# A state-space scan with decays from summed rows in DRAM, a channel-wise y, and z's weights in another slot

## The reference, cut to what matters

```python
y_f = ssd_scan(xs, dtl[:, :, 0], a[0], bf, cf, hf_ctx)
y_b = ssd_scan(xs[:, ::-1], dtl[:, ::-1, 1], a[1], bb[:, ::-1], cb[:, ::-1], hb_ctx)[:, ::-1]
y = y_f + y_b + d_skip[layer][:, None] * xs
y = y.reshape(bsz, n, D_INNER)
y_ssd = rmsnorm(y * jax.nn.silu(z), ssd_norm_w[layer]) @ w_ssd_out[layer]
```

## Time and profile before

| | us |
|---|---|
| median of 3 runs | 3327.76 (3324.04 to 3328.95) |
| span of the profiled execution | 3323.6 |
| scan's loop in it, first conv product to f_in's first | 71.40 to 739.23 |

### The profile page before, as it was taken

The page is one execution under the profiler, slowest core; times in us unless marked ns, Lnnn a source line. Parts: engine busy times, 40 slices in busy tenths (PEclk is TensorE's granted clock), DMA queues, the critical chain, the costliest instruction groups (busy, mean ns, idle before and its releaser), DMA issues.

```text
span 3323.6 us, 40435 instructions
## 1 busy us (share of the span) xinstructions
PE 3186.9 (96%) x13834; PEld 1884.2 (57%) x13835; DVE 1355.6 (41%) x2174; ACT 730.8 (22%) x1302; POOL 393.2 (12%) x312
## 2 busy tenths in 40 slices
PE   7999999999999999999999999999899999999999
PEld 5555555556488743333333333333587788888887
DVE  2544545464434532122221222212457477555451
ACT  3212131312021111111111111111314354311100
POOL 0212222222100100000000000000201244100000
PEclk9999999999999999999999999999899999999999
DMA  4121212134612369999999999879412121222111
GB/s 203 56 77 57 76 52 81 47 107 160 218 73 76 137 258 374 384 394 388 393 382 381 392 389 355 324 285 368 147 51 105 42 78 56 86 76 89 64 76 54
DMA packets 185079, 615.71 MB, mean 185 GB/s; under 512 B 18176, under 2 KB 55168, under 8 KB 174240
## 3 DMA queue, kind: packets, MB, share of 16 engines
q1 hardware_dynamic: 161216, 552.79, 43.6%
q0 software_dynamic: 10944, 39.85, 3.3%
q10 hardware_dynamic: 12832, 21.88, 1.8%
HBM read 578.01 MB, written 36.44 MB: 185 GB/s over the span
## 4 chain that ended last, share of the span: by engine, by line
PE 85%; DMA 6%; DVE 5%; issue 1%; ACT 1%; SPq 1%; POOL 0%; ACTq 0%; DVEq 0%; POOLq 0%
PE ps L322 24%; PE ps L2273 16%; PE ps L2247 11%; PE ps L1940 9%; PE ps L271 6%; DMA slot<-in_w_exp 5%; PE ps L2011 3%; PE ps L2502 2%; PE ps L2027 2%; PE ps L1986 2%; PE ps L2032 1%; PE ps L2474 1%; PE ps L2457 1%; PE ps L2242 1%; PE ps L2238 1%
## 5 line engine op out<-in xcount | busy, mean ns | idle before, releaser
L2273 PE MATMUL ps<-slot,xT_blk 128*64 128x512 f32 x3200 | 733.8, 599 | 28.8 <-DMA slot<-in_w_exp 26.4
L2273 PEld LDWEIGHTS ps<-slot,xT_blk 128*64 128x64 f32 x3200 | 217.9, 137 | 465.6 <-issue 376.4
L2247 PE MATMUL ps<-slot,aT 128*64 128x512 f32 x1632 | 363.8, 598 | 0.9 <-ACT aT L1638 0.9
L1940 PE MATMUL ps<-hT,slot 128*128 128x512 f32 (+1 forms) x896 | 307.6, 501 | 1.1 <-ACT small L1435 1.1
L2247 PEld LDWEIGHTS ps<-slot,aT 128*64 128x64 f32 x1632 | 117.5, 138 | 239.4 <-issue 239.4
L3007 DVE TENSOR_TENSOR gate<-ps,b_row 128x512 f32<-128x512 f32 x50 | 34.6, 692 | 513.1 <-PE ps L2273 512.6
L1940 PEld LDWEIGHTS ps<-hT,slot 128*128 128x128 f32 x896 | 168.0, 190 | 129.8 <-issue 120.9
L2628 DVE SCALAR_TENSOR_TENSOR conv<-ps,g_conv,conv 128x510 f32<-128x510 f32 (+1 forms) x224 | 133.3, 631 | 193.2 <-ACT conv L1448 189.8
L3003 DVE MEMSET b_there<- 128x1 f32 x50 | 3.0, 59 | 391.8 <-DMA b_few<-in_b_gu 383.0
L322 PE MATMUL ps<-in_t,in_s 128*128 128x264 f32 x528 | 124.7, 386 | 0.5 <-issue 0.5
L2011 PE MATMUL ps<-hT,slot 128*128 128x512 f32 x256 | 121.5, 620 | 0.0
(11 more groups left out here) (509 smaller groups left out, 4792.4 us busy)
## 6 DMA issues: line engine op xcount, KB each, us to landing
slot<-in_w_exp SPq DMA_DIRECT2D x768, 512.0 KB, 9.2
in_w<-in_w_ffn SPq DMA_DIRECT2D x22, 1024.0 KB, 4.8
expert_rows<-zero SPq DMA_DIRECT2D x4, 4608.0 KB, 22.6
slot<-in_w_xbc SPq DMA_DIRECT2D x8, 2048.0 KB, 26.4
w_modT<-in_w_modT POOLq DMA_DIRECT2D x32, 512.0 KB, 3.5
rnn_w<-in_w_rnn SPq DMA_DIRECT2D x16, 1024.0 KB, 4.8
expert_rows<-y_row ACTq DMA_DIRECT2D x102, 128.0 KB, 5.6
out_w<-in_w_ffn_out SPq DMA_DIRECT2D x8, 1408.0 KB, 8.2
```

The lines of the kernel that those rows point to most:

```text
L1940: last = pe.matmul(ps[:, 2 * (m % 2) + part, 0:n], w[:, (k * 4 + m % 4) * P:(k * 4 + m % 4 + 1) * P], hT[:, k, c0:c0 + n], start=(k == 0), ...
L2247: last = pe.matmul(ps[h * UNIT:(h + 1) * UNIT, 6, :], aT[:, t, d * UNIT:(d + 1) * UNIT], slot[4 + d][:, t * D + h * 512:t * D + (h + 1) * ...
L2273: last = pe.matmul(ps[h * UNIT:(h + 1) * UNIT, 2 * s + t, :], xT_blk[:, k, s * UNIT:(s + 1) * UNIT], slot[i // 4][:, at:at + 512], start=( ...
```

## The change

- The decays. TensorE makes, once, the running sums S as rows (8 matmuls, [64 heads x 512 tokens], step `rows`); VectorE copies them to SBUF; ScalarE's queue stores them with 8 DMAs in the DRAM tensor sum_rows. For each chunk ScalarE's queue loads one row of 1024 values to all 128 partitions (`load_sums`, 512 KB into sum_here, two buffers, two chunks ahead). GpSimd adds a mask that is 0 or -1e30 (`row`), and ScalarE takes, for each of the 8 heads, exp of 128 columns with the bias -S_s (`decay`). `segment`, da_upto and cb_masked are gone; VectorE multiplies decay by cb straight from PSUM.
- The carried term. ScalarE takes exp of sum_here in one 1024-wide instruction (`into`), VectorE multiplies it by C for all 8 heads (`scaled`).
- The output. Both terms of all 8 chunks are written by channels: for each head 64 columns of the state or of x_dt are the weights, 128 columns of c_into or decay move, and the result goes to one half of the partitions of banks 4 to 7, where the two directions and both terms are summed in PSUM. The steps on y_part and y_tok, GpSimd's skip and the 16 transposes are gone; at the end VectorE does y = x times skip + PSUM, and y times silu(z), four times each (silu of x is kept by channels in xT).
- z's weights go to the slot that conv0 to conv3 used, after conv3; z0 comes whole ahead of the states, and the rest is spread unevenly: half a tile in each of chunks 0 to 4, a quarter in 5 and 6, none in 7. The loop over groups becomes one over pairs of groups on SyncE and TensorE, as the slots alternate.
- The second direction's first two states come in chunk 3, the rest in chunk 4; scaled(j+1) and masked(j+1) follow those of j on VectorE without any y step between.

```diff
         with act.Fori(0, GROUPS) as g:
+            def load_sums(j):
+                d, _, t = CHUNKS[j]
+                act.dma_start(sum_here[j % 2][:].rearrange("p h l -> p (h l)"),
+                              sum_rows[bass.ds(g * (2 * TT) + (d * TT + t), 1), :].partition_broadcast(P)).then_inc(s_row[j % 2], 16)
+            load_sums(0)
+            load_sums(1)
...
             def decays(j):
-                ssd_pe.after(act, f"segment{j}", g)
-                ssd_act.done(act.activation(decay[j % 2][:].rearrange("p (q h) l -> p q (h l)", q=2), ps[:, 0:2, :],
-                                            ACT.Exp), f"decay{j}")
+                act.wait_ge(s_row[j % 2], g * 64 + (16 * (j // 2) + 16))
+                if j >= 2:
+                    ssd_pe.after(act, f"carried{j - 2}", g)
...
+                ssd_act.done(act.activation(c_into[j % 2][:], sum_here[j % 2][:], ACT.Exp), f"into{j}")
+                ssd_pool.after(act, f"row{j}", g)
+                for h in range(HPG):
+                    last = act.activation(decay[j % 2][:, h, :], decay[j % 2][:, h, :], ACT.Exp, bias=g_small[:, MINUS_SUM, t, d, h:h + 1])
+                ssd_act.done(last, f"decay{j}")
+                if j < 6:
+                    ssd_act.after(act, f"into{j}", g)
+                    load_sums(j + 2)
...
+            def into_y(j, left, right, first):
+                t = CHUNKS[j][2]
+                for h in range(HPG):
+                    half = slice(h % 2 * HD, (h % 2 + 1) * HD)
+                    last = pe.matmul(ps[half, Y_BANK + h // 2, t * P:(t + 1) * P], left[:, h * HD:(h + 1) * HD], right[:, h, :],
+                                     start=first, stop=True, skip_group_check=not first)
+            z_piece(0, 0, 1)
             states(0, [0, 1])
-            segment(0)
+            scores(0)
             states(0, [2, 3, 4])
             for j in range(8):
+                states(1, STATES_AT.get(j, []))
+                for piece in Z_PIECES[j]:
+                    z_piece(*piece)
+                ssd_dve.after(pe, f"scaled{j}", g)
+                ssd_dve.after(pe, f"state{d}_{i + 1}", g)
+                ssd_pe.done(into_y(j, state[:, i, :], c_into[j % 2], j == 0), f"carried{j}")
+                if j < 7:
+                    scores(j + 1)
                 ssd_dve.after(pe, f"masked{j}", g)
                 ssd_pool.after(pe, f"x_dt{d}", g)
-                for h in range(HPG):
-                    last = pe.matmul(ps[:, 6, h * HD:(h + 1) * HD], decay[j % 2][:, h, :], x_dt[:, t, h * HD:(h + 1) * HD],
...
+                ssd_pe.done(into_y(j, x_dt[:, t, :], decay[j % 2], False), f"diagonal{j}")
...
+            def weigh(j):
+                ssd_dve.done(dve.tensor_tensor(c_into[j % 2][:], c_into[j % 2][:], over_heads(cT[:, d, t * P:(t + 1) * P]), ALU.mult), f"scaled{j}")
+                ssd_pe.after(dve, f"cb{j}", g)
+                ssd_act.after(dve, f"decay{j}", g)
+                ssd_dve.done(dve.tensor_tensor(decay[j % 2][:], decay[j % 2][:], over_heads(ps[:, 2, 0:P]), ALU.mult), f"masked{j}")
+            states(0, [0, 1])
+            weigh(0)
+            states(0, [2, 3, 4])
...
+            def sums(j):
+                pool.wait_ge(s_row[j % 2], g * 64 + (16 * (j // 2) + 16))
+                if j >= 2:
+                    ssd_pe.after(pool, f"diagonal{j - 2}", g)
...
+                ssd_pool.done(pool.tensor_tensor(decay[j % 2][:], sum_here[j % 2][:],
+                                                 never[:, d, :].unsqueeze(1).broadcast_to([P, HPG, P]), ALU.add), f"row{j}")
```

More of the change, by code:

```diff
@@ L79 @@
 CHUNK = KD * 4 * P
+NEVER = -1e30
 class Steps:
@@ L629, in program @@
     zT = area("zT", [P, 4, SEQ])
+    sum_here = [area(f"sum_here{i}", [P, HPG, P]) for i in range(2)]
+    never = area("never", [P, 2, P])
     CHUNKS = [(d, i, i if d == 0 else TT - 1 - i) for d in range(2) for i in range(TT)]
@@ L1914, in _ @@
             heads = slice(d * N_HEADS, (d + 1) * N_HEADS)
-            last = pe.matmul(into_psum[:, :, heads], cst[:, CST[into]], small[:, DA, :, heads], start=True, stop=True)
-        dt_pe.done(last, "into")
+            last = pe.matmul(sum_psum[:, :, heads], cst[:, CST[into]], small[:, DA, :, heads], start=True, stop=True)
+        dt_pe.done(last, "sum")
         dt_pe.done(pe.matmul(over_psum, ones, small[:, DA], start=True, stop=True), "over")
+        mods_dve.all(pe)
+        for d, into in enumerate(["le", "ge"]):
+            heads = slice(d * N_HEADS, (d + 1) * N_HEADS)
+            for t in range(TT):
+                last = pe.matmul(ps[heads, 6, t * P:(t + 1) * P], small[:, DA, t, heads], cst[:, CST[into]], start=True, stop=True)
+        dt_pe.done(last, "rows")
         norm1.act.all(pe)
@@ L2000, in _ @@
                 d, i, t = CHUNKS[j]
-                if j == 4:
-                    states(1, [0, 1])
-                if j == 0:
-                    segment(1)
-                if j == 0:
-                    pe.wait_ge(w_loaded[1], g * 32 + (ssd_first[1] + 32))
-                elif j % 2 == 0:
-                    ssd_act.after(pe, f"z{j // 2 - 1}", g)
-                for k in range(4 * (j % 2), 4 * (j % 2) + 4):
-                    last = pe.matmul(ps[:, 3, :], slot[1][:, (k * 4 + j // 2) * P:(k * 4 + j // 2 + 1) * P],
-                                     hT[:, k, 0:SEQ], start=(k == 0), stop=(k == KD - 1))
@@ L2029, in _ @@
-                ssd_pe.done(last, f"diagonal{j}")
-                ssd_dve.after(pe, f"state{d}_{i + 1}", g)
-                ssd_pe.done(pe.matmul(ps[:, 7, :], cT[:, d, t * P:(t + 1) * P], state[:, i, :], start=True, stop=True),
-                            f"carried{j}")
-            last_t = CHUNKS[7][2]
-            def turn_y(m, t):
-                return pe.transpose(ps[:, Y_BANKS[m], t * P:(t + 1) * P], y_tok[:, t, m * P:(m + 1) * P], ident)
-            ssd_dve.after(pe, "y6", g)
-            ssd_act.after(pe, "z3", g)
@@ L2600, in _ @@
         dt_dve.done(dve.tensor_tensor(small[:, DT_END], small[:, DT_END], small[:, DT], ALU.mult), "end")
+        dt_pe.after(dve, "sum")
+        dt_dve.done(dve.tensor_scalar(small[:, MINUS_SUM], sum_psum, -1.0, None, ALU.mult), "minus_sum")
+        dt_pe.after(dve, "rows")
+        dt_dve.done(dve.tensor_copy(sum_row[:], ps[0:2 * N_HEADS, 6, :]), "rows")
         ssd_dve.open(dve)
@@ L2634, in fade, with states @@
                 ssd_dve.done(dve.tensor_tensor(by_head(y_part[:]), by_head(src), per_head(OVER, tile, d), ALU.mult), name)
-            def states(d):
+            def states(d, which):
                 order = STATES[d]
-                ssd_pe.after(dve, f"state{d}_0", g)
-                fade(d, ps[:, 4, :], order[1], f"state{d}_0")
-                for i in range(1, 5):
+                for i in which:
+                    if i == 0:
+                        ssd_pe.after(dve, f"state{d}_0", g)
+                        fade(d, ps[:, 0, :], order[1], f"state{d}_0")
+                        continue
+                    ssd_dve.after(dve, f"state{d}_{i - 1}", g)
```

320 lines of the change are left out of this document (172 added, 148 removed).

## The result

The changed kernel takes 3248.18 us (median of 4 runs, 3247.21 to 3249.92), the kernel before 3326.16 beside it; the ratio is 0.9766, with a 95% interval of 0.9752 to 0.9779. The forecast was 3243, with 3214 to 3286 as its range. The span is the time from the first to the last instruction of the profiled execution: 3245.4 us, 78.2 less than before.

What follows compares the result with a forecast made beforehand. TensorE bound the chunks (68.28 of 69.20 us busy), waits the head. Four groups of 144.5 us save 89.8; minus 1.9 and 3.5, 84.4: span 3323.6 becomes 3239.2, median 4.2 above: 3243 us, range 3214 to 3286.

Steps and rivals of the forecast that it cites:

- The terms with 64-column weights: Diagonal and carried terms on TensorE: 256 passes per group at 0.070 us, 17.9 us; ends 13.7 and 27.6.
- the rival of ideal overlap: Column halves overlap fully, a pass costs 0.054 us and the waits vanish: 34 us less, 3209; chance 0.08.
- the rival without overlap: Column halves don't overlap at 128 columns, a pass costs 0.108 us: 9.7 us more per group, 3282; chance 0.13.
- A floor of 62 ns a pass: Skill's sequencer floor per matmul in one decode mode; would make the terms 15.9 us and the time 3235.
- Switches: TensorE changing between weight shapes: about 30 per group at 0.155 us, 4.7 us; lower end half of it.
- The head: Start of each group's chunk phase: z0 covers the first old wait; PE idles 2.9 us for state0_4 behind weigh(0).
- Other small waits: Per group, 1.5 us added for scaled1 and masked1, ready about level with PE's need, and for small waits.
- The buffer loop: sum_here reloaded after decay(j): landing 4.1 us, 8.9 for two chunks, 4.5 each; taken as hidden behind PE.
- The rival with queueing row loads: Row loads queue in the chunks; slower than before from a landing of 17.7 us, 3393 at 22.6; chance 0.05.
- The waits-rival: In the chunks, GpSimd/VectorE blocking or row loads landing in twice 4.1 us: 16 to 32 us more, 3267 middle; chance 0.18.
- The sum: Per group 79.7 + 60.4 + 2.9 + 1.5 = 144.5 us; four are 578.0 against 667.8, 89.8 off.
- Start and end: Outside the group loop: rows step adds 1.9 us at the start, f_in's wait for y and gate steps 3.5 at the end.

Runs made afterwards that it cites:

- the run with all five edits: Changed kernel with straight TensorE loop, VectorE's head fade first, second-direction states early, cb after the diagonal term, z's last half whole in chunk 6: 3224.46 us, ratio 0.9700.

## Why the prediction was right, point by point

- **TensorE's work is time, until another engine is next.** Right: 86.3 us became 63.2, and TensorE still sets the pace.
- **The terms with 64-column weights.** I took 0.070 a pass between 0.054 and 0.108. Without the changes of shape it is 0.055, 14.0 us a group instead of 17.9: the overlap was the right reason, as the run with the halves in another order shows, and it is whole. The weight load, for which I had put the price up, hides behind it. So the rival of ideal overlap had the pass right and only the vanishing waits wrong, and the rival without overlap falls; its 0.108 is what one half alone shows. A floor of 62 ns a pass is not there in these runs, with two passes in 0.109 us.
- **Switches.** 0.155 each and 4.7 us a group were right, with 0.18 and 4.9 measured for 28, but by luck. The experts' row holds two switches for its 0.16, not one. What hid the slip is that the time between starts shows only a part of them: cb between two terms takes 0.42 (170.62 to 171.04) instead of 0.22 alone (160.49 to 160.71), 0.20 for two, and another 0.15 stands in the terms on its two sides. (The expectations of the runs read the switch as 0.10 and the pass as 0.064; the sum is the same.)
- **The head.** z0 as cover is right (without it 36 us are lost), and so is what is late next: PE waits for the state behind weigh(0), 2.52 us where I had 2.9. Most of it goes when the order of VectorE is turned.
- **Other small waits.** 1.5 us were priced for carried1 and small things; they came elsewhere: 0.98, 0.94 and 0.99 in chunks 4 and 7, 0.28 at a z copy, 3.2 in all, and about 0.8 more that TensorE loses around its five waits beyond the idle time itself. I had called the chunks hidden with a microsecond or two to spare; in chunk 4 I counted the states on TensorE but not that VectorE takes their first fade after masked4.
- **The buffer loop.** Right: landing 3.6 us in the median (4.1 assumed), 8.5 the longest of 32, and 2.3 us more cost nothing. GpSimd waited for a row load only four times, and for TensorE 24 times. The rival with queueing row loads falls: no landing comes near the 17.7 us from which it decides.
- **GpSimd and VectorE.** The waits-rival had the right mechanism and a small part of its price. scaled took 2.24 us in the median and 4.78 at the longest, against 1.22 alone, but TensorE seldom waited for it. A row took 2.35 us, not 1.9 to 2.0.
- **The sum.** Group 1 took 142.9 us against 144.5: 3.9 less for the passes, 0.2 more for switches, 2.1 more for waits. Four such groups would be 6.4 us under the sum, but the loop took 584.7 against 578.0, 6.7 over it. The step that failed is that the loop over pairs on TensorE was costed at nothing: it cost 8.2 us at the one jump back (6.28 of standing and 1.9 in conv0). Two more terms were missing: TensorE's lower clock behind the head's wait in groups 3 and 4 (3.3 us), and at the end p1's wait of 1.35 for z's silu. With the loop written straight it is 574.4, 3.6 under the sum. That the total is off by only 5 us is in part luck: the pass was priced 16 us too high over four groups, and what was left out is 13. Start and end were 0.8 and 4.1 us against 1.9 and 3.5, which tests nothing, as both vary by more from run to run; but p2 waits 3.43 us for the gate steps, as laid out.

## What to carry to other kernels

Two products with 64 columns of weights that write to alternate halves of the partitions overlap fully even with 128 moving columns, so a result laid out by channels can be summed in PSUM where it was added and transposed before. What takes back part of it is each change of weight shape: keep products of one shape together, if no wait grows by it. At the head of a phase whose first elementwise results are late, a product that depends on nothing can be worth more than its own time (here 8 us a group for 6.9 of work); ask what it covers before it is moved. A loop whose body is doubled to alternate two buffers can cost time at the jump, here 8 us: look at the first instruction after it, and try the loop written out straight. And when a kernel's time agrees with a sum, check the sum's terms one by one: here two large errors nearly cancelled.

## What the runs showed of the hardware

- TensorE's jump back is free with a body of 1104 products and weight loads. With one of 2208 or more it costs 4.1 to 6.5 us of standing in the traces here, and 7 to 8 us of time.
- A pass of 128 columns with 64-column weights takes 0.109 us on one half, and a pass on the other half runs beside it (pairs 0.007 us apart, 0.055 a pass). A change between 64- and 128-column weights adds 0.18.
- VectorE's product of two SBUF operands waits for GpSimd's instruction to end (4.11 instead of 0.69 us), and GpSimd's is held up by it in turn (x_end 5.46 instead of 4.48). The masked step, with one operand in PSUM, took 1.21 or 1.22 us all 32 times in the changed kernel, and the same beside x_end (166.20, in the run with all five edits).
- After a wait of 2.5 us TensorE ran at the lower clock in one group and not in another: z's half behind it took 3.60 us in the first group, 5.29 in the third and 4.25 in the fourth (granted clock 0.72 there). In the straight version, with the same wait, it took 3.60 in all four. What decides between them wasn't tried.
